# The 2-D Fourier stage of a hybrid diffusion step: the first step's result stays on the chip, channel by channel

## What is computed

```python
def fourier_mix(u):
    b, s, w = u.shape
    ug = u.reshape(b, s, N_FOURIER, w // N_FOURIER).astype(jnp.float32)
    f = jnp.fft.fftn(ug, axes=(1, 3), norm='ortho').real
    return f.reshape(b, s, w).astype(u.dtype)
```

## Time and profile before

| | |
|---|---|
| time, median of 3 executions | 2885.48 us (2882.11 to 2888.46) |
| the profiled execution's own time | 2884.65 us |
| span of its trace | 2882.9 us |
| granted TensorE clock, mean | 0.956 of full speed |
| PE busy | 2549.0 us, 88% of the span |
| Fourier stage in the trace | SP's first transfer at 2306.55 us, output stage's first at 2432.36 us |

### The profile page before, as it was taken

The page is one execution under the profiler, slowest core; times in us unless marked ns, Lnnn a source line. Parts: engine busy times, 40 slices in busy tenths (PEclk is TensorE's granted clock), DMA queues, the critical chain, the costliest instruction groups (busy, mean ns, idle before and its releaser), DMA issues. The chain is left out here.

```text
span 2882.9 us, 53072 instructions
## 1 busy us (share of the span) xinstructions
PE 2549.0 (88%) x18772; PEld 2050.2 (71%) x18772; DVE 1261.2 (44%) x2644; ACT 971.1 (34%) x1991; POOL 795.0 (28%) x1273
## 2 busy tenths in 40 slices
PE   3899999999999689999999577888888754899999
PEld 1688888888888578888888456666666622688887
DVE  2534434343443243333333145665666511666665
ACT  2444444444444332222222134544545411211110
POOL 2223333332333200000000134434444300444442
PEclk8999999999999889999999789999999978899999
DMA  7433333333333342222222488876777599666664
GB/s 286 139 108 113 116 121 102 117 120 106 115 115 104 112 168 100 95 95 95 95 95 88 108 175 182 180 163 157 167 164 167 122 282 245 219 205 206 206 205 143
DMA packets 286657, 425.19 MB, mean 147 GB/s; under 512 B 45045, under 2 KB 203029, under 8 KB 282795
## 3 DMA queue, kind: packets, MB, share of 16 engines
q1 hardware_dynamic: 273132, 389.25, 47.3%
q10 hardware_dynamic: 12831, 32.85, 3.3%
q0 software_dynamic: 544, 1.09, 0.2%
HBM read 288.74 MB, written 134.34 MB: 147 GB/s over the span
## 5 line engine op out<-in xcount | busy, mean ns | idle before, releaser
L258 PE MATMUL p_ps_m<-p_w_hi,p_h_hi 128*128 128x512 f32 x1904 | 771.1, 405 | 20.3 <-DVE p_h_lo L768 19.5
L259 PE MATMUL p_ps_m<-p_w_lo,p_h_hi 128*128 128x512 f32 x1904 | 750.7, 394 | 0.0
L260 PE MATMUL p_ps_m<-p_w_hi,p_h_lo 128*128 128x512 f32 x1904 | 749.1, 393 | 0.0
L258 PEld LDWEIGHTS p_ps_m<-p_w_hi,p_h_hi 128*128 128x128 f32 x1904 | 359.2, 189 | 99.5 <-issue 20.3
L260 PEld LDWEIGHTS p_ps_m<-p_w_hi,p_h_lo 128*128 128x128 f32 x1904 | 358.8, 188 | 80.5
L259 PEld LDWEIGHTS p_ps_m<-p_w_lo,p_h_hi 128*128 128x128 f32 x1904 | 359.5, 189 | 72.6
L258 PE MATMUL o_ps_y<-o_w_hi,o_y_hi 128*128 128x512 f32 x544 | 218.4, 401 | 9.7 <-DVE o_y_lo L1744 9.7
L259 PE MATMUL o_ps_y<-o_w_lo,o_y_hi 128*128 128x512 f32 x544 | 218.2, 401 | 0.0
L260 PE MATMUL o_ps_y<-o_w_hi,o_y_lo 128*128 128x512 f32 x544 | 214.5, 394 | 0.0
L1267 PE MATMUL a_ps_o<-a_v_win,a_p_t 128*64 128x64 f32 x2112 | 94.2, 230 | 100.8 <-DMA a_kv<-s_kv 39.8
L1267 PEld LDWEIGHTS a_ps_o<-a_v_win,a_p_t 128*64 128x64 f32 x2112 | 77.1, 140 | 138.6 <-issue 89.9
(11 more groups left out here) (202 smaller groups left out, 4469.7 us busy)
## 6 DMA issues: line engine op xcount, KB each, us to landing
p_xr<-in_x_sample SPq DMA_DIRECT2D x64, 512.0 KB, 3.9
p_xt<-in_x_sample_t SPq DMA_DIRECT2D x64, 512.0 KB, 4.6
a_scan<-s_scan SPq DMA_DIRECT2D x68, 258.0 KB, 5.6
s_scan<-p_w_raw SPq DMA_DIRECT2D x136, 128.0 KB, 2.4
a_kv<-s_kv SPq DMA_DIRECT2D x68, 256.0 KB, 6.3
a_v_win<-s_p SPq DMA_DIRECT2D x132, 128.0 KB
o_x<-in_x_sample SPq DMA_DIRECT2D x32, 512.0 KB, 4.9
out_y_sample<-o_y ACTq DMA_DIRECT2D x32, 512.0 KB, 4.4
```

The costliest lines, as they stand in the source:

```text
L258: pe.matmul(out, left_hi(k), right_hi(k), start=(k == 0), stop=False)
L259: pe.matmul(out, left_hi(k), right_lo(k), start=False, stop=False)
L260: last = pe.matmul(out, left_lo(k), right_hi(k), start=False, stop=(k == K8 - 1))
```

## The change

The changed stage loads all of `g` for the grid into the chip at once, as two halves of 128 channels (`x[0]`, `x[1]`). The real parts go to partitions 0 to 63 on SP's queue and the imaginary parts to 64 to 127 on ACT's, in pieces of 512 bytes; then SP loads the whole of `dft_second`. The roles of the operands in the first step are turned round: the stationary operand is now the data of one channel, 64 columns that lie 128 elements (512 bytes) apart in `x`, and the moving operand is a half of `first`, 64 columns. Each channel takes two matmuls, the first to PSUM partitions 0 to 63 (real part of the result), the second to 64 to 127 (imaginary part). So b is on the partitions of PSUM already, as the second step needs it, and nothing goes through DRAM: `y1` is gone. Eight channels fill a bank of 512 columns, and ACT and DVE copy the 32 banks in turn, contiguously, into `mid`, which is ordered by channel and then k1. The second step reads `mid[:, :, k1]` as moving operand: 256 columns that lie 64 elements (256 bytes) apart. Its results go in turn to PSUM partitions 0 to 63 and 64 to 127, four k1 to a bank, so that there are 16 banks to copy. SP stores each pair of banks with two transfers of 64 partitions. All loops are written out. The prompt's part is as before.

```diff
-def fourier_groups(eng):
-
-    with eng.Fori(1, 3) as n:
-        for s in range(4):
-            yield n * 4 - 4 + s, s
-
-
 def fourier_stage(nc, io, keep):
 
 
 
-    GW = 8
-    BANKS = GW // 2
+    CH = W_GRP // 2
+    PER = 8
+    FILLS1 = W_GRP // PER
+    FILLS2 = 64 // 4
+    GROUPS = FILLS2 // 2
+    BANKS = 6
     SLOTS = 4
     with stage(nc) as (ctx, new_sem):
         sb = lambda name, shape, dt=F32: ctx.enter_context(nc.sbuf_tensor("f_" + name, shape, dt))
         sem = lambda name: new_sem("f_" + name)
         first = sb("first", [P, P])
-        second = [sb(f"second{s}", [P, GW, 64]) for s in range(SLOTS)]
-        gx = [sb(f"gx{s}", [P, GW, W_GRP]) for s in range(SLOTS)]
-        yx = [sb(f"yx{s}", [P, GW, W_GRP]) for s in range(SLOTS)]
+        second = sb("second", [P, 64, 64])
+        x = [sb(f"x{h}", [P, 64, CH]) for h in range(2)]
+        mid = sb("mid", [P, W_GRP, 64])
+        yx = [sb(f"yx{s}", [P, 4, W_GRP]) for s in range(SLOTS)]
         whole = sb("whole", [P, 2, 2, N_PROMPT])
         gp = sb("gp", [P, 2, 2, W_GRP])
         yp = sb("yp", [P, 2, W_GRP])
-        ps = [ctx.enter_context(nc.psum_tensor(f"f_ps{b}", [P, 2, W_GRP], F32)) for b in range(BANKS)]
+        ps = [ctx.enter_context(nc.psum_tensor(f"f_ps{b}", [P, 512], F32)) for b in range(BANKS)]
         ps_p = ctx.enter_context(nc.psum_tensor("f_psp", [P, 2, W_GRP], F32))
...
+        gv = io["g"][:, 0:N_GRID, :].rearrange("r (a b) c -> r a b c", b=64)
+        yv = io["yc"][0:N_GRID, :].rearrange("(k2 k1) c -> k2 k1 c", k1=64)
+
+        def evict_mid(copy, n):
+
+            return copy(mid[:, n * PER:(n + 1) * PER, :], ps[n % BANKS][:, :].rearrange("p (c k) -> p c k", k=64))
+
+        def evict_out(copy, n, m):
+
+            return copy(yx[m // 2 % SLOTS][:, m % 2 * 2:m % 2 * 2 + 2, :], ps[n % BANKS][:, :].rearrange("p (j c) -> p j c", j=2))
 
         @block.sync
         def _(sp):
-            sp.dma_start(first[:, :], io["dft_first"]).then_inc(consts, 16)
-            gv = io["g"][:, 0:N_GRID, :].rearrange("r (a b) c -> r a b c", b=64)
-            for i, s in fourier_groups(sp):
-                ahead(sp, i * BANKS + BANKS, i * (GW * W_GRP * 4))
-                sp.wait_ge(mm[0], i * BANKS + BANKS)
-                for r in range(2):
-                    sp.dma_start(gx[s][64 * r:64 * r + 64, :, :], gv[r, :, bass.ds(i * GW, GW), :]).then_inc(slot_in[0][s], 16)
+            sp.dma_start(first[:, :], io["dft_first"]).then_inc(first_in, 16)
+            for h in range(2):
+                sp.dma_start(x[h][0:64, :, :], gv[0, :, :, h * CH:(h + 1) * CH]).then_inc(x_in[h], 16)
+            sp.dma_start(second[:, :, :], io["dft_second"]).then_inc(second_in, 16)
+            for m in range(GROUPS):
+                for e in range(2):
+                    sp.wait_ge(freed[e], FILLS1 // 2 + m + 1)
+                for z in range(2):
+                    sp.dma_start(yv[:, 8 * m + 4 * z:8 * m + 4 * z + 4, :], yx[m % SLOTS][64 * z:64 * z + 64, :, :]).then_inc(sent[m % SLOTS], 16)
             for s in range(SLOTS):
-                sp.wait_ge(sent[0][s], 48)
-            yv = io["y1"].rearrange("(r k) b c -> r b k c", r=2)
-            for i, s in fourier_groups(sp):
-                ahead(sp, i * BANKS + BANKS, i * (GW * W_GRP * 4 * 64), i * (GW * 64 * 4))
-                sp.wait_ge(mm[1], i * BANKS + BANKS)
-                for r in range(2):
-                    sp.dma_start(gx[s][64 * r:64 * r + 64, :, :], yv[r, :, bass.ds(i * GW, GW), :]).then_inc(slot_in[1][s], 16)
-                sp.dma_start(second[s][:, :, :], io["dft_second"][:, bass.ds(i * GW, GW), :]).then_inc(slot_in[1][s], 16)
+                sp.wait_ge(sent[s], 32 * (GROUPS // SLOTS))
 
         @block.gpsimd
         def _(pool):
...
 
         @block.tensor
         def _(pe):
-            for q in range(2):
-                pe.sem_inc(mm[q], SLOTS * BANKS)
-            pe.wait_ge(consts, 16)
-            for q in range(2):
-                for i, s in fourier_groups(pe):
-                    pe.wait_ge(slot_in[q][s], (i - s) * (4 * (2 + q)) + 16 * (2 + q))
-                    for n in range(BANKS):
-
-                        pe.wait_ge((by_act, by_dve)[n % 2][q], i * (BANKS // 2) + n // 2 + 1)
-                        if q == 0:
-                            last = pe.matmul(ps[n][:, :, :], first[:, :], gx[s][:, 2 * n:2 * n + 2, :], start=True, stop=True)
-                        else:
-                            for k in range(2):
-                                last = pe.matmul(ps[n][0:64, k, :], second[s][:, 2 * n + k, :], gx[s][:, 2 * n + k, :], start=True, stop=True)
-                        last.then_inc(mm[q], 1)
+            pe.wait_ge(first_in, 16)
+            for n in range(FILLS1):
+                if n % (FILLS1 // 2) == 0:
+                    pe.wait_ge(x_in[n // (FILLS1 // 2)], 32)
+                if n >= BANKS:
+                    pe.wait_ge(freed[n % 2], (n - BANKS) // 2 + 1)
+                for q in range(PER):
+                    c = n * PER + q
+                    for z in range(2):
+                        last = pe.matmul(ps[n % BANKS][64 * z:64 * z + 64, q * 64:(q + 1) * 64], x[c // CH][:, :, c % CH],
+                                         first[:, 64 * z:64 * z + 64], start=True, stop=True)
+                last.then_inc(filled, 1)
+            pe.wait_ge(second_in, 16)
+            for e in range(2):
+                pe.wait_ge(freed[e], FILLS1 // 2)
+            for m in range(FILLS2):
+                n = FILLS1 + m
+                pe.wait_ge(freed[n % 2], (n - BANKS) // 2 + 1)
+                for j in range(2):
+                    for z in range(2):
+                        k1 = 8 * (m // 2) + 4 * z + m % 2 * 2 + j
+                        last = pe.matmul(ps[n % BANKS][64 * z:64 * z + 64, j * W_GRP:(j + 1) * W_GRP], second[:, k1, :], mid[:, :, k1],
+                                         start=True, stop=True)
+                last.then_inc(filled, 1)
             pe.wait_ge(gp_in, 64)
             for kc in range(2):
                 for r in range(2):
...
 
         @block.scalar
         def _(act):
-            for q in range(2):
-                act.sem_inc(by_act[q], BANKS // 2)
-                for s in range(SLOTS):
-                    act.sem_inc(sent[q][s], 16)
-            for q in range(2):
-                rows = slice(0, P if q == 0 else 64)
-                for i, s in fourier_groups(act):
-                    act.wait_ge(sent[q][s], (i - s) * 4 + 16)
-                    for n in range(0, BANKS, 2):
-                        act.wait_ge(mm[q], i * BANKS + n + SLOTS * BANKS + 1)
-                        act.activation(yx[s][rows, 2 * n:2 * n + 2, :], ps[n][rows, :, :], ACT.Copy).then_inc(by_act[q], 1)
-                    act.wait_ge(by_act[q], i * (BANKS // 2) + BANKS)
-                    act.wait_ge(by_dve[q], i * (BANKS // 2) + BANKS)
-                    if q == 0:
-                        act.dma_start(io["y1"][:, bass.ds(i * GW, GW), :], yx[s][:, :, :]).then_inc(sent[q][s], 16)
-                    else:
-                        act.dma_start(io["yc"][0:N_GRID, :].rearrange("(k2 k1) c -> k2 k1 c", k1=64)[:, bass.ds(i * GW, GW), :],
-                                      yx[s][rows, :, :]).then_inc(sent[q][s], 16)
+            for h in range(2):
+                act.dma_start(x[h][64:P, :, :], gv[1, :, :, h * CH:(h + 1) * CH]).then_inc(x_in[h], 16)
+            copy = lambda to, src: act.activation(to, src, ACT.Copy)
+            for n in range(0, FILLS1, 2):
+                act.wait_ge(filled, n + 1)
+                evict_mid(copy, n).then_inc(freed[0], 1)
+            for m in range(0, FILLS2, 2):
+                act.wait_ge(filled, FILLS1 + m + 1)
+                if m // 2 >= SLOTS:
+                    act.wait_ge(sent[m // 2 % SLOTS], 32 * (m // 2 // SLOTS))
+                evict_out(copy, FILLS1 + m, m).then_inc(freed[0], 1)
             act.wait_ge(yp_mm, 1)
             act.activation(yp[:, :, :], ps_p[:, :, :], ACT.Copy).then_inc(yp_sb, 1)
             act.wait_ge(yp_sb, 1)
             act.dma_start(io["yc"][N_GRID:N_TOK, :].rearrange("(j p) c -> p j c", p=P), yp[:, :, :]).then_inc(yp_sent, 16)
             act.wait_ge(yp_sent, 16)
-            for s in range(SLOTS):
-                act.wait_ge(sent[1][s], 48)
 
         @block.vector
         def _(dve):
-            for q in range(2):
-                dve.sem_inc(by_dve[q], BANKS // 2)
-            for q in range(2):
-                rows = slice(0, P if q == 0 else 64)
-                for i, s in fourier_groups(dve):
-                    dve.wait_ge(sent[q][s], (i - s) * 4 + 16)
-                    for n in range(1, BANKS, 2):
-                        dve.wait_ge(mm[q], i * BANKS + n + SLOTS * BANKS + 1)
-                        dve.tensor_copy(yx[s][rows, 2 * n:2 * n + 2, :], ps[n][rows, :, :]).then_inc(by_dve[q], 1)
+            for n in range(1, FILLS1, 2):
+                dve.wait_ge(filled, n + 1)
```

(6 more changed lines are left out.)

13 lines of the change are left out of this document (6 added, 7 removed).

## The result

| | before | after |
|---|---|---|
| median of 20 executions each | 2889.34 us | 2893.89 us |
| lowest and highest | 2882.11, 2896.53 | 2889.78, 2902.20 |
| ratio to before, 95% interval | | 1.0024 (1.0015 to 1.0033) |
| the profiled execution's own time | 2884.65 us | 2892.77 us |
| Fourier stage: SP's first transfer to the output stage's first | 125.8 us | 130.0 us |

The changed kernel is slower, by 0.24% by the ratio (0.15 to 0.33%) and by 4.6 us or 0.16% by the two medians. The 0.2% that were named as what can be told from no change lie inside that interval, so the loss is small and at the edge of what can be told. The forecast was 2839. The stage itself became 4.2 us longer; it begins at 2306.5 to 2320.1 us in the traces of this study, because the unchanged stages ahead vary, so stages are compared by their length.

The account below looks back on a forecast made before the run. The prediction took DMA transfers to bound the stage before, PE after. Its terms ended the stage at 2387 instead of 2432.4, 45.4 us less: 2839 us from 2884.65, range 2830 to 2873.

Parts of the forecast that it names:

- (1): Stage start: loading the first half x[0] takes 20.5 us, plus 2 us for issue and landing; PE begins at 2329.8.
- (3): First step: 1024 records at 31 ns, 31.7 us, plus 1.8 us cold start and 0.8 us last copy; ends 2364.2.
- (4): Second step on PE: 128 records of 256 columns, halves overlapping, 0.111 us each, 14.2 us, ending at 2378.4.
- (5): End of stage: prompt's matmuls 3.7 us, then copy, store and barrier 3.7 us, giving 2385.8; with stores, 2387 taken.
- The stationary read at double: First step: the stationary read costs double, 62 ns a record, 63.5 us; kernel 2871 us; chance 0.17.
- slower case: First step: stationary loads double and halves on one column lose overlap, 124 ns a record; kernel 2935 us; chance 0.08.
- deciding point of 75: First step: the slower case decides from 75 ns a record on, (45.4 + 31.7) us / 1024.
- loses the overlap: Second step: moving read at steps of 256 bytes loses the halves' overlap, 0.222 us a record; kernel 2852 us; chance 0.12.
- both at double: Both steps: 62 ns and 0.222 us a record, stage end 2431.8, kernel 2884 us, no measurable change; chance 0.05.
- cold start: First step: PE's clock was at 0.50 before, about 3.6 us at 1.2 GHz, adding 1.8 us.
- ACT held by its issues: First step: ACT's load issues hold it to about 2344, PE loses 6.4 us; kernel 2846 us; chance 0.04.

Follow-up runs that it names:

- the first experiment: Changed kernel with the first step's stationary operand read contiguously, which changes what is computed: median 2857.23 us, ratio to before 0.9892.
- the sweep in turn: Changed kernel with stationary steps of 1 to 129 elements and moving steps of 1 to 64, PSUM halves in turn: one execution, 2886.05 us.
- the last experiment: Changed kernel with the two halves of the first step on different channels, 16 bytes apart: median 2876.22 us, ratio to before 0.9952.

## Why the prediction was wrong, by its steps

The stage from the issue of the first load to its end was forecast as 79.7 us (2307.3 to 2387), and took 129.6 (2311.90 to 2441.51); before it took 125.1. By the terms:

| step | forecast | measured | difference |
|---|---|---|---|
| (1) first half in, PE begins | 22.5 | 18.9 | -3.6 |
| (3) first step | 33.5 | 74.6 | +41.1 |
| (3) last copy | 0.8 | 1.0 | +0.2 |
| (4) second step | 14.2 | 27.8 | +13.6 |
| (5) prompt, stores, barrier | 8.6 | 7.4 | -1.2 |

**The step that failed** is the last paragraph of (3): "so I take the step as free here". It carried the price of a stepped read from DVE to PE because both take an element at about the same pace. On PE the read goes by 16-byte lines, and both operands of the change have one element in a line: 59 ns a stationary record at such a step and 0.216 us a moving one, against 29 to 30 ns and 0.11 us contiguous. The row was DVE's, and no row of PE stood beside it. Whether a step is nearly free even on DVE stays open: the 8% rest on the assumption of one cycle an element, and the 585 ns of the stepped copy have no contiguous copy from SBUF beside them. In (4) the step was not priced at all, and there it cost 13.6 us more.

**The rivals.** The stationary read at double gave 62 ns; step 4 alone gives 59.4, so it was right and came with more: 11 to 17 ns for the halves on one column, which no rival had as a small cost. The rival that the prediction made its slower case had this conflict, as a full loss of the overlap at 124 ns; the measured 73 ns is just under its deciding point of 75, and the cost that it named was there, but small: 17 ns and not 62. That point was worked out with the second step at 14.2 us; with 27.8 the same sum puts it at 62, (45.4 - 13.6 + 31.7) us / 1024, and the kernel is past it. The moving read "loses the overlap" at 0.222 us had the right price for the second step (0.217) and the wrong mechanism; "both at double", 2884, was the nearest and took its second step from it, so in that half its nearness is luck. In the stage it was 5.1 us short (124.5 against 129.6): 9.3 too little in the first step (74.6 against 63.5 + 1.8 us), and 3.6 too much at the start, which made up for a part of it. The total is 9.9 us off because the median before, 2889.34, is also 4.7 us above the execution from which it was reckoned. It had 0.05 of the chance.

**What was right.** The transfers were the bound, and once the first half of `x` is in they are off the path. The halves do overlap: 58.4 ns in one half against 29.2 in turn. The pace of contiguous records: 31 ns against 29.2 to 30.4, and 0.111 against 0.110 us. The cold start was taken as 1.8 us: with the contiguous stationary operand the first piece is 8.34 us for 212 records, 1.9 us more than at 30.4 ns. With both reads contiguous the stage came within 1.1 us of the forecast, but not by the same terms: PE starts 2.4 us earlier than forecast, and the first step, with PE's stops (1.57 and 2.65 us), takes 37.8 us instead of 33.5. (1) was too high by 3.6 us: the windows show 348 to 354 GB/s, 64 partitions on SP's queue and 64 on ACT's, where SP's alone, also 64 partitions at a time, had 218; the estimate took the middle between 218 and 310. The Trainium skill (SBUF — State Buffer, "Can I just issue two DMAs to hit both halves?") states a gain of 6% for two transfers at once. Here the rate is 60% higher, and for this pattern the measurement decides; but the pieces differ too (512 bytes against 8 KB), and no run separates the one from the other.

**ACT held by its issues** didn't happen. The timeline of ACT:

```profile
2311.52 10.51 ACTq L1511 DMA_DIRECT2D f_x<-s_g  x2
2333.44 0.61 ACT L1512 ACTIVATE f_mid<-f_ps 128x512 f32<-128x512 f32 x1 [27.44 <-PE f_ps L1485]
```

The issues took 10.5 us and were over at 2322, 9 us before PE began; the first copy waited only for its bank.

**Left open.** What the stops of "issue" are (4.3 us in the first experiment, 4.2 with both steps contiguous, 2.5 in the sweep in turn); the changed kernel shows none. In all three kernels they come at the same place, after 212 records and again after 126 or 128 more, although these 128 took 3.95 us in two of them and 6.56 us in the sweep. So they go by the place in the program and not by the time. The profile has a queue called "instruction", and one of its packets falls in the 3 us before each resumption (2342 to 2343 and 2349 to 2350 in the first experiment, where PE resumes at 2344.75 and 2351.78). That the instructions come late, behind the loads, fits this, but it is an argument, and no run tested it. Why runs of eight matmuls a half cost 87 ns, between the 56 of halves on different columns and the 111 of one half, was not followed further, nor why the changed kernel has 72 to 73 ns where the sweep has 70.3.

## What to carry to other kernels

On TensorE the layout of an operand is part of its price: elements four or more float32 apart were read at half the pace or less here, stationary or moving, and the price is paid by every record. Let the copy out of PSUM do the rearranging, as long as it lies under something. Of the stepped copies measured here, 512 elements each, a read on DVE was the cheapest (585 ns, against 1.02 to 1.09 us for a write on DVE and for either on ACT). And a cost carried over from another engine's row, however alike the paces, is a bound of the range and not its middle.

## What the runs showed of the hardware

**The stepped read does not follow PE's clock.** In the changed kernel PE has 30 records (PEld 31) in 2 us at a granted clock of 0.50 (2331 to 2333) and 31 (PEld 31) at 1.00 (2337 to 2339), in the windows above. In the kernel with the contiguous stationary operand, 2 us hold 43 at 0.50 and 76 at 1.00:

```profile
2337.00:2339.00 2.00, 2.00 (x43) 2.00 (x42) 0.06 (x1) 0.60 (x1) 0.00 (x0) 0.50 1.15 348
2355.00:2357.00 2.00, 2.00 (x76) 2.00 (x74) 0.69 (x1) 0.60 (x1) 0.00 (x0) 1.00 0.00 0
```

The loads are not the reason, though they ran in the first window and not in the second: from 2340 to 2342, at 1.00 and 348 GB/s, 77 stand in 2 us. The moving read at a step of 64 is alike: in the last experiment the windows of 2 us hold 12 records of the second step each, at 0.50 (2391 to 2393) as at 1.00 (2400 to 2402).

**Two kinds of stride.** With the halves of PSUM in turn and both on the same column, stationary steps of 64 and 128 elements cost 70 to 73 ns where 129 costs 59; with different columns 56. In one half alone there is no such surcharge (111 against 117). For the moving operand it is the same: 0.287 us at step 64 on the same addresses, 0.216 at the same step 16 bytes apart. At 32 a part of it shows already (0.248).
